# Latent mixer: who settles the steps of a bisection, and who copies one transposed piece in four

## The chip, the cores and the metric

One Trainium2 chip, one of its cores. The metric is the device time of one execution in microseconds; lower is better. TensorE multiplies and transposes, VectorE (DVE), ScalarE (ACT) and GpSimd (POOL) work on tiles of 128 partitions, and SyncE (SP) issues transfers here. Each engine runs its own list of instructions in order; semaphores order them between engines. GpSimd reads SBUF alone, the other three read PSUM too.

## The reference

One inference step of a two-layer encoder for a prompt of 1024 frames and a sample of 64 frames over a cache of 256. Layer 0 has two head groups side by side: A, attention over keys that an indexer selects, and B, multi-head latent attention. What matters here:

```python
def mla_core(k_nope, k_rope, v, k_pos, q_nope, q_rope, q_pos):      # group B, the latent mixer
    logits = (einsum('bqhd,bshd->bhqs', q_nope, k_nope)
              + einsum('bqhd,bsd->bhqs', q_rope, k_rope)) * (B_NOPE + B_ROPE) ** -0.5
    logits = where(chunk_mask(q_pos, k_pos)[None, None], logits, -inf)
    p = softmax(logits, axis=-1)
    return einsum('bhqs,bshd->bqhd', p, v)                          # 8 heads, k_nope and v = latent @ w_ukv

def dsa_core(...):                                                  # group A
    idx_score = einsum('bqhs,bqh->bqs', relu(sc), wi)               # masked
    _, sel = top_k(idx_score, topk)                                 # 256 of up to 1024 keys
    ...                                                             # attention over the selected keys
```

## The kernel before

The program is a row of stages, one behind the other: the projection of layer 0, the indexer's scores, the latent mixer (`attention` with kind "b", tiles `att_b_...`), the sparse mixer ("a"), output projection, the two halves of the feed-forward block, and then layer 1. A stage begins when the one before it has ended on all engines.

**Units.** The latent mixer works through 36 units: four pairs of heads, and in each pair nine query tiles t = 0 to 8. Tile t < 8 has 128 queries and 128 (t + 1) keys; tile 8 is the sample, 64 queries and 320 keys. A unit's width is its number of keys, so t = 4 to 7, with five to eight blocks of 128 keys, are the wide units. Per unit and head:

- TensorE computes the scores into PSUM (`scores`, L1128), three units ahead (`ahead` = 3).
- VectorE masks them, copies them to `prob` and takes the row's extreme (`peak`, L1362).
- ScalarE takes the exponential with its sum (`exponential`, L1291).
- VectorE takes the reciprocal of the sum (`over_sum`, L1385).
- GpSimd scales the row by it in place (L1103), which is the normalising.
- TensorE transposes the row, block by block, into one of three PSUM banks (`piece`, L1167): group 0 is blocks 0 to 3, group 1 blocks 4 to 7. The order in a unit is group 0 of head 0, group 0 of head 1, group 1 of head 0, group 1 of head 1. A piece waits until the piece three places before it has been copied out.
- An engine copies each piece to SBUF (`copy_piece`, L1226 on ScalarE, tile `pt`). `copier` says who: for the latent mixer always ScalarE.
- TensorE multiplies with the values (`products`, L1196) for the unit before, and ScalarE takes the result away (`output`, L1281).

During a pair TensorE also expands the next pair's keys and values from the latents (`expand`, L1147 and L1151, kind "x"), through the same three banks, in order behind the unit's transposed pieces; ScalarE copies those with even numbers and VectorE those with odd numbers. The last pair has none.

**The search.** The indexer's scores of six query tiles (t = 2 to 7) lie in SBUF, and the sparse mixer needs for each row the value of its 256th largest. It is found by bisection on the bits of a float: 32 steps, spread over the first 30 units by `search_steps`, one to a unit and two in units 16 and 25 (t = 7 of the second and the third pair, the doubled units). In a step VectorE counts for three tiles how many scores lie below the candidate (L1417, 896, 768 and 512 columns), and ScalarE for the other three by a sum of signs (L1298, 1024, 640 and 384 columns). `settle` then compares six counts per partition with their limits, keeps the candidate's bit or not, and writes the next candidate (L1424, L1427, L1432, all 128x6). The next count on both engines waits for `cand_ready`. VectorE's order in a unit is: over_sum(i + 1, head 1), in a doubled unit the first count, two peaks for unit i + 3, in a doubled unit the first settling, its expanded pieces, the count, over_sum(i + 2, head 0), settle. ScalarE's is: output, copies of group 0, an exponential, in a doubled unit the first count, copies of group 1, an exponential, its expanded piece, the count. GpSimd has nothing but the normalising, head 0 and then head 1.

**The tail.** From unit 30 on VectorE turns the bits found into thresholds and masks (`next_float`, `room_for_ties`, `select`), and works through four of the six tiles in units 32 to 35.

## Time and profile before

| what | us |
|---|---|
| median of 3 runs | 3007.72 (3005.83 to 3008.99) |
| the profiled execution | 3008.22 |
| its span | 3006.4 |
| TensorE busy | 2833.9 (94%) |
| VectorE busy | 2018.3 (67%) |
| ScalarE busy | 1412.2 (47%) |
| GpSimd busy | 532.4 (18%) |

The shares are averages over all stages. The change touches one stage, so the whole program's shares say little about it: its own windows have to be read. A time of the timeline counts from the span's start. "Idle before" in a row is the time the engine stood still ahead of that instruction, with what ended it. The ends of matrix multiplications are modelled, and the durations of GpSimd are rough; distances between starts are firmer.

### The profile page before, as it was taken

How to read it: one execution, taken by the hardware profiler on the slowest of the kernel's cores; microseconds unless marked ns; L12 is line 12 of the kernel's file. 1: busy time of each engine (PE TensorE's matmuls, PEld its weight loads, DVE VectorE, ACT ScalarE, POOL GpSimd, SP SyncE). 2: the span in 40 equal slices, each digit the busy share in tenths (PEclk: the TensorE clock that was granted, in tenths of full speed). 3: DMA queues.
4: the chain of work that ended last, by engine and by line, in shares of the span. 5: the costliest groups of instructions: out<-in, count | busy, mean ns of one | idle time of the engine just before them, and what ended most of it. 6: DMA issues, size and time to landing. Idle time of an engine off the chain costs nothing. (4 is left out here: it accounts for less than half of the span.)

```text
span 3006.4 us, 49479 instructions
## 1 busy us (share of the span) xinstructions
PE 2833.9 (94%) x18462; PEld 2368.9 (79%) x18462; DVE 2018.3 (67%) x3648; ACT 1412.2 (47%) x2850; POOL 532.4 (18%) x410
## 2 busy tenths in 40 slices
PE   8986997999999999899999899999899999999998
PEld 6762564668899999788799566865688999998787
DVE  5447999865867776677631565139857777767777
ACT  5335996552444344433243455348724444444333
POOL 0000222420011110465000231000000111114551
PEclk9996999999999999999999999999999999999999
DMA  4111001021233323654411201120112333326442
GB/s 154 46 36 29 14 14 50 2 65 67 75 97 104 107 97 96 235 172 129 168 51 46 92 2 53 56 77 2 58 74 61 101 109 99 104 91 227 154 130 103
DMA packets 203120, 259.04 MB, mean 86 GB/s; under 512 B 27100, under 2 KB 132180, under 8 KB 202900
## 3 DMA queue, kind: packets, MB, share of 16 engines
q1 hardware_dynamic: 202900, 256.10, 25.8%
q8 instruction: 139, 2.28, 0.3%
q14 instruction: 81, 0.66, 0.1%
HBM read 177.90 MB, written 77.64 MB: 85 GB/s over the span
## 5 line engine op out<-in xcount | busy, mean ns | idle before, releaser
L247 PE MATMUL X<-up_th,high 128*128 128x272 f32 x1232 | 356.4, 289 | 4.1 <-ACT up_U L2287 2.9
L249 PE MATMUL X<-up_th,low_r 128*128 128x272 f32 x1232 | 355.2, 288 | 0.0
L247 PEld LDWEIGHTS X<-up_th,high 128*128 128x128 f32 x1232 | 232.2, 188 | 8.3 <-ACT up_U L2287 6.1
L2248 POOL TENSOR_TENSOR up_sum<-up_U 128x512 f32<-128x512 f32 x20 | 33.4, 1669 | 1131.9 <-DVE up_U L2399 1131.9
L249 PEld LDWEIGHTS X<-up_th,low_r 128*128 128x128 f32 x1232 | 231.9, 188 | 0.0
L2381 DVE SCALAR_TENSOR_TENSOR up_cv<-up_G,tap,up_cv 128x1024 f32<-128x1024 f32 (+1 forms) x176 | 130.3, 782 | 136.9 <-ACT up_cv L2296 135.3
L247 PE MATMUL up_x<-up_th,up_high 128*128 128x272 f32 x704 | 202.9, 288 | 1.4 <-DVE up_low_r L1859 1.4
L249 PE MATMUL up_x<-up_th,up_low_r 128*128 128x272 f32 x704 | 203.7, 289 | 0.0
L248 PE MATMUL X<-sums_r,high 128*128 128x272 f32 x528 | 152.0, 288 | 0.0
L247 PE MATMUL up_y<-up_th,up_high 128*128 128x272 f32 x528 | 151.9, 288 | 0.0
L249 PE MATMUL up_y<-up_th,up_low_r 128*128 128x272 f32 x528 | 151.6, 287 | 0.0
L2795 DVE TENSOR_TENSOR xres<-X,xres 128x1024 f32<-128x1024 f32 x80 | 97.4, 1222 | 72.1 <-PE X L249 72.1
L247 PE MATMUL X<-w_hi_p_r,a_hi_p_r 128*128 128x512 f32 x352 | 137.9, 392 | 0.0
L249 PE MATMUL X<-w_hi_p_r,a_lo_p_r 128*128 128x512 f32 x352 | 137.8, 391 | 0.0
L248 PE MATMUL X<-w_lo_p_r,a_hi_p_r 128*128 128x512 f32 x352 | 137.7, 391 | 0.0
L247 PEld LDWEIGHTS up_x<-up_th,up_high 128*128 128x128 f32 x704 | 132.9, 189 | 1.8 <-DVE up_low_r L1859 1.8
L2692 ACT ACTIVATE w_hi_p_r<-b_f 128x1024 fp32r<-128x1024 f32 x54 | 57.0, 1056 | 161.0 <-POOL b_f L2751 41.9
L249 PEld LDWEIGHTS up_x<-up_th,up_low_r 128*128 128x128 f32 x704 | 132.5, 188 | 0.0
L2770 DVE TENSOR_TENSOR a_lo_p_r<-a_lo_p_f,a_hi_p_r 128x1024 fp32r<-128x1024 f32 x64 | 107.6, 1689 | 10.6 <-ACT a_hi_p_r L2696 10.6
L1859 DVE TENSOR_TENSOR up_low_r<-up_low,up_high 128x1024 fp32r<-128x1024 f32 (+1 forms) x66 | 109.9, 1664 | 1.3 <-ACT up_high L1849 0.6
L1849 ACT ACTIVATE up_high<-up_low 128x1024 fp32r<-128x1024 f32 (+1 forms) x66 | 79.2, 1203 | 64.2 <-DVE up_low L1840 64.2
L2736 POOL TENSOR_TENSOR w_lo_p_r<-b_f,w_hi_p_r 128x1024 fp32r<-128x1024 f32 x38 | 102.2, 2692 | 37.1 <-ACT w_hi_p_r L2692 37.0
(581 smaller groups left out, 8665.6 us busy)
## 6 DMA issues: line engine op xcount, KB each, us to landing
scratch_a<-up_U SPq DMA_DIRECT2D x44, 544.0 KB, 2.7
low<-in_w_up_dram SPq DMA_DIRECT2D x44, 512.0 KB, 5.1
up_low<-in_w_up_dram SPq DMA_DIRECT2D x44, 512.0 KB, 4.9
scratch_s<-up_sum SPq DMA_DIRECT2D x80, 256.0 KB, 2.0
b_f<-in_w_down_dram SPq DMA_DIRECT2D x40, 512.0 KB, 4.4
a_lo_p_f<-scratch_s SPq DMA_DIRECT2D x40, 512.0 KB, 4.2
a_lo_p_f<-scratch_a SPq DMA_DIRECT2D x30, 512.0 KB, 4.5
scratch_att<-out_x SPq DMA_DIRECT2D x16, 512.0 KB, 2.6
```

Source lines behind the costliest of these rows:

```text
L247: nc.tensor.matmul(out, lh, rh, start=first, stop=False, skip_group_check=on_top)
L248: nc.tensor.matmul(out, lh, rl, start=False, stop=False, skip_group_check=on_top)
L249: return nc.tensor.matmul(out, ll, rh, start=False, stop=last, skip_group_check=on_top)
L1849: nc.scalar.activation(high[:, j0:j1], raw[:, j0:j1], ACT.Copy).then_inc(hi, 1)
L1859: nc.vector.tensor_tensor(low[1][:, j0:j1], low[0][:, j0:j1], high[:, j0:j1].bitcast(F32), ALU.subtract).then_inc(lo, 1)
L2248: g.tensor_tensor(t0, a21, a22, ALU.add).then_inc(pair_summed, 1)
L2381: last = v.scalar_tensor_tensor(cv[:, t0:t0 + n], G[m % 2][:, g0 + j:g0 + j + n], tap[:, j * NF + m:j * NF + m + 1], cv[:, t0:t0 + n], ALU ...
L2692: s_.activation(slots.split(f"w_hi_{what}"), w_source(what), ACT.Copy).then_inc(w_hi, 1)
L2736: g.tensor_tensor(slots.split(f"w_lo_{what}"), w_source(what), slots.high(f"w_hi_{what}"), ALU.subtract).then_inc(w_lo_pool, 1)
L2770: v.tensor_tensor(slots.split(f"{x}_lo_{what}"), of, slots.high(f"{x}_hi_{what}"), ALU.subtract).then_inc(lo, 1)
L2795: v.tensor_tensor(xs, bank[:, 2 * h:2 * h + 2, :], xs, ALU.add).then_inc(added, 1)
```

## The change

`settle` moves from VectorE's list to GpSimd's. There it follows the normalising of the next unit: behind the two scalings of unit i stand the settlings of the steps of unit i - 1. The exclusive-or, the predicated copy and the shift to a constant are replaced by arithmetic: the difference between limit and count (`room`, in the tile `ok`) is compared with zero, the result is multiplied by a signed step `flip` and added to `bits`, `flip` is halved, and the next candidate is `bits` plus `flip`. After the first step that is six instructions of 128x6 instead of three. The first step sets `bits` and `flip` in its own way. `settled` counts four a step instead of two, a semaphore `flipped` and a tile `flip` are new, and VectorE waits for the last settling before `next_float`.

In `copier`, for the latent mixer, the piece of head 1 and group 1 goes to VectorE: the last transposed piece of every wide unit. In VectorE's list these copies are the first instruction of the unit, ahead of over_sum(i + 1, head 1).

```diff
--- before.py
+++ after.py
@@ -977,7 +977,9 @@
 
         if what == "x":
             return "dve" if j % 2 else "act"
-        if mla or stick:
+        if mla:
+            return "dve" if (x, j) == (1, 1) else "act"
+        if stick:
             return "act"
         return "act" if x == 0 else "dve"
 
@@ -995,7 +997,8 @@
             below = sb("below", [P, wide[-1]], BF16)
             up = sb("up", [P, n_top], mybir.dt.int32)
             counted = {"dve": sem("counted_dve"), "act": sem("counted_act")}
-            settled, cand_ready = sem("settled"), sem("cand_ready")
+            flip = sb("flip", [P, n_top], mybir.dt.int32)
+            settled, cand_ready, flipped = sem("settled"), sem("cand_ready"), sem("flipped")
         if mla or dsa:
             top, work, spare, told = src["top"], src["work"], src["top"]["spare"], sem("told")
             scratch = below if mla else sb("scratch", [P, 2 * SEQ], BF16)
@@ -1094,6 +1097,31 @@
                     for h in range(2):
                         g.memset(left[s][h][:, SEQ:SEQ + 1], 1.0).then_inc(cleared, 1)
                 return
+            def settle(step):
+
+                for by, n in (("dve", BY_DVE), ("act", n_top - BY_DVE)):
+                    pool.wait_ge(counted[by], FROM + n * (step + 1))
+                room = top["ok"][:].bitcast(F32)
+                g.tensor_tensor(room, top["limit"][:], top["cnt"][:], ALU.subtract).then_inc(settled, 1)
+                pool.wait_ge(settled, FROM + 4 * step + 1)
+                if step:
+                    g.tensor_scalar(top["cand"][:], room, 0.0, None, ALU.is_ge).then_inc(settled, 1)
+                    pool.wait_ge(settled, FROM + 4 * step + 2)
+                    g.tensor_tensor(top["cand"][:], top["cand"][:], flip[:], ALU.mult).then_inc(settled, 1)
+                    pool.wait_ge(settled, FROM + 4 * step + 3)
+                    g.tensor_tensor(top["bits"][:], top["bits"][:], top["cand"][:], ALU.add).then_inc(settled, 1)
+                    if step + 1 < STEPS:
+                        g.tensor_scalar(flip[:], flip[:], 0.5, None, ALU.mult).then_inc(flipped, 1)
+                else:
+                    g.tensor_scalar(top["bits"][:], room, 0.0, 1.0, ALU.is_ge, ALU.subtract).then_inc(settled, 2)
+                    g.tensor_scalar(flip[:], room, 0.0, 2.0, ALU.is_ge, ALU.mult).then_inc(settled, 1)
+                    pool.wait_ge(settled, FROM + 4)
+                    g.tensor_scalar(flip[:], flip[:], 1.0, float(1 << 30), ALU.subtract, ALU.mult).then_inc(flipped, 1)
+                if step + 1 < STEPS:
+                    pool.wait_ge(settled, FROM + 4 * step + 4)
+                    pool.wait_ge(flipped, FROM + step + 1)
+                    g.tensor_tensor(top["cand"][:], top["bits"][:], flip[:], ALU.add).then_inc(cand_ready, 1)
+
             for i, (p, t) in enumerate(order):
                 n, w = queries(t), key_tile(t)[0]
                 for h in range(2):
@@ -1101,6 +1129,9 @@
                     c = 2 * (i % ring) + h
                     pool.wait_ge(rcp_done[h], FROM + i + 1)
                     g.tensor_scalar(pr, pr, rr[0:n, c:c + 1], 1.0, ALU.mult, ALU.mult).then_inc(prob_ready[h], 1)
+                if mla and i:
+                    for step in SEARCH_AT[i - 1]:
+                        settle(step)
 
         @block.tensor
         def _(pe):
@@ -1417,20 +1448,6 @@
                     v_.tensor_scalar(below[:, wide[j]:wide[j + 1]], w[:], top["cand"][:, j:j + 1].bitcast(F32), None, ALU.is_lt, ALU.add,
                                      accum_out=top["cnt"][:, j:j + 1]).then_inc(counted["dve"], 1)
 
-            def settle(step):
-
-                for by, n in (("dve", BY_DVE), ("act", n_top - BY_DVE)):
-                    dve.wait_ge(counted[by], FROM + n * (step + 1))
-                v_.tensor_tensor(top["ok"][:], top["cnt"][:], top["limit"][:], ALU.is_le).then_inc(settled, 1)
-                dve.wait_ge(settled, FROM + 2 * step + 1)
-                if step:
-                    v_.copy_predicated(top["bits"][:], top["ok"][:], top["cand"][:]).then_inc(settled, 1)
-                else:
-                    v_.tensor_scalar(top["bits"][:], top["ok"][:], 1.0, None, ALU.subtract).then_inc(settled, 1)
-                dve.wait_ge(settled, FROM + 2 * step + 2)
-                if step + 1 < STEPS:
-                    v_.tensor_scalar(top["cand"][:], top["bits"][:], 1 << (30 - step), None, ALU.bitwise_xor).then_inc(cand_ready, 1)
-
             def not_above(columns):
                 for j in columns:
                     w = work[SEARCHED[j]]
@@ -1517,8 +1534,6 @@
                 if i + ahead < n_units:
                     for h in range(2):
                         peak(i + ahead, h)
-                if mla and len(SEARCH_AT[i]) > 1:
-                    settle(SEARCH_AT[i][0])
                 if i:
                     pieces_of(dve, "dve", i, "x")
                     if not mla:
@@ -1531,9 +1546,8 @@
                     count_below(SEARCH_AT[i][-1])
                 if i + 2 < n_units:
                     over_sum(i + 2, 0)
-                if mla and SEARCH_AT[i]:
-                    settle(SEARCH_AT[i][-1])
                 if mla and i == SEARCH_ENDS + 1:
+                    dve.wait_ge(settled, FROM + 4 * STEPS)
                     next_float()
                 if mla and i == SEARCH_ENDS + 2:
                     room_for_ties()
```

## Rows read from the trace of the kernel before

**Rows 1.** Windows of the search and the tail, all engines, busy us (instructions).
```profile
308.00:476.20 168.20, 152.36 (x1014) 97.15 (x1013) 160.04 (x476) 166.71 (x446) 42.02 (x58) 0.98 0.05 13
...
476.20:508.00 31.80, 23.95 (x226) 16.33 (x224) 31.17 (x68) 16.60 (x43) 9.45 (x10) 1.00 0.00 1
```

**Rows 2.** Waits of ScalarE in the search: us in total, times, longest.
```profile
ACT att_b_k L1226 <- PE att_b_tp L1147: 1.0, 3, 0.7
```

**Rows 3.** Timeline, first count end and count starts: start us, duration us.
```profile
311.56 0.08 DVE L1417 DVE_READ_ACCUMULATOR att_b_below<-scores,top_cand 128x1 f32 x1
...
312.76 1.15 ACT L1298 ACTIVATE att_b_below<-scores,top_cand 128x1024 bf16<-128x1024 f32 x1
...
393.16 1.14 ACT L1298 ACTIVATE att_b_below<-scores,top_cand 128x1024 bf16<-128x1024 f32 x1
...
397.19 1.15 ACT L1298 ACTIVATE att_b_below<-scores,top_cand 128x1024 bf16<-128x1024 f32 x1
...
401.07 1.15 ACT L1298 ACTIVATE att_b_below<-scores,top_cand 128x1024 bf16<-128x1024 f32 x1
...
405.70 1.18 ACT L1298 ACTIVATE att_b_below<-scores,top_cand 128x1024 bf16<-128x1024 f32 x1
...
409.91 1.18 ACT L1298 ACTIVATE att_b_below<-scores,top_cand 128x1024 bf16<-128x1024 f32 x1
```

**Rows 4.** Timeline of step 12, VectorE and GpSimd.
```profile
375.36 1.13 DVE L1417 TENSOR_SCALAR_CACHE_REDUCE att_b_below<-scores,top_cand 128x896 bf16<-128x896 f32 x1
...
378.02 0.07 DVE L1417 DVE_READ_ACCUMULATOR att_b_below<-scores,top_cand 128x1 f32 x1
...
378.26 0.93 POOL L1103 TENSOR_SCALAR att_b_prob<-att_b_prob,att_b_rr 128x768 f32<-128x768 f32 x1 [4.48 <-DVE att_b_rr L1385]
...
378.53 0.68 DVE L1432 TENSOR_SCALAR top_cand<-top_bits 128x6 int32<-128x6 int32 x1
```

**Rows 5.** Groups of GpSimd (busy us, mean ns, idle), then its timeline.
```profile
L1103 POOL TENSOR_SCALAR att_b_prob<-att_b_prob,att_b_rr 128x128 f32<-128x128 f32 x8 | 3.0, 376 | 29.4 <-DVE att_b_rr L1385 29.4
...
L2759 POOL TENSOR_TENSOR b_f<-b_f,b_f 128x1024 f32<-128x1024 f32 x10 | 24.0, 2396 | 0.0
...
L3099 POOL MEMSET const-float32-1.0<- 128x1 f32 x1 | 0.1, 98 | 0.0
...
820.92 1.66 POOL L2248 TENSOR_TENSOR up_sum<-up_U 128x512 f32<-128x512 f32 x1 [177.70 <-DVE up_U L2399]
...
822.73 1.56 POOL L2251 TENSOR_TENSOR up_sum<-up_sum,up_U 128x512 f32<-128x512 f32 x1
...
826.40 1.29 POOL L2257 TENSOR_TENSOR up_sum<-up_U 128x512 f32<-128x512 f32 x1 [0.42 <-DMA scratch_s<-up_sum]
```

**Rows 6.** Timeline of the second pair's unit with five blocks.
```profile
370.59 0.32 ACT L1298 ACTIVATION_READ_ACCUMULATOR att_b_below<-scores,top_cand 128x1 f32 x1
...
372.98 0.80 POOL L1103 TENSOR_SCALAR att_b_prob<-att_b_prob,att_b_rr 128x640 f32<-128x640 f32 x1 [0.17 <-DVE att_b_rr L1385]
...
374.03 1.09 PE L1167 MATMUL att_b_tp<-ident,att_b_prob 128*128 128x128 f32 x8
```

**Rows 7.** Copies of transposed pieces: timeline of ScalarE, group of VectorE (sparse mixer).
```profile
399.74 1.07 ACT L1226 ACTIVATE att_b_pt<-att_b_tp 128x512 f32<-128x512 f32 x2
...
L1250 DVE COPY att_a_pt<-att_a_tp 128x512 f32<-128x512 f32 x24 | 16.3, 680 | 5.2 <-PE att_a_tp L1167 5.2
```

**Rows 8.** Timeline of the first pair's unit with eight blocks.
```profile
346.71 0.15 DVE L1385 RECIPROCAL att_b_rr<-att_b_rs 64x1 f32<-64x1 f32 x1
...
346.82 0.66 PE L1167 MATMUL att_b_tp<-ident,att_b_prob 128*128 128x128 f32 x4 [0.56 <-ACT att_b_pt L1226]
...
348.50 0.69 DVE L1237 COPY att_b_v<-att_b_tp 128x512 f32<-128x512 f32 x1 [0.84 <-PE att_b_tp L1151]
```

**Rows 9.** Timeline at the end of the search.
```profile
474.52 0.26 ACT L1298 ACTIVATION_READ_ACCUMULATOR att_b_below<-scores,top_cand 128x1 f32 x1
...
476.09 0.08 DVE L1417 DVE_READ_ACCUMULATOR att_b_below<-scores,top_cand 128x1 f32 x1
```

## The prediction

> **What bounds the kernel now.** The change lies inside one stage, the latent mixer, which runs from about 298 to 508 us; the stages before and after it keep their instructions, so its length is all that can move. I cut the stage by windows first. While the search runs (308 to 476 us) ScalarE is busy 166.71 of 168.20 us and VectorE 160.04, GpSimd only 42.02 [rows 1]. In the tail (476 to 508) ScalarE is half idle and VectorE is busy 31.17 of 31.80 us [rows 1]. The list of waits says the same in another way: through the search ScalarE's longest entry is 1.0 us in three waits, for TensorE's block of expanded keys that it copies, and it never waited for a candidate [rows 2]. So ScalarE's own work sets the pace of the search, VectorE comes close behind, and the tail is VectorE's alone.
>
> Then I read the search step by step. Both engines count against one candidate, the step is settled, and both count again. The starts of ScalarE's first count in five successive steps, 393.16 to 409.91 [rows 3], are the loop. From the unit with seven blocks into the doubled unit they are 4.03 us apart, inside it 3.88, then 4.63 and 4.21; 168 us for 31 intervals make 5.4 on average. The reader is to see that these four intervals are short: they leave little between the end of one count and the start of the next for anything that must happen in between.
>
> **Settling.** Removed from VectorE: three instructions a step, 96 in all less one. In step 12 the last read of the count starts at 378.02 and the candidate write, held up beside a normalising instruction of GpSimd (378.26 to 379.19), ends at 379.21 [rows 4]: 1.1 us from the end of a count to a candidate, less where the normalising is narrow. VectorE sheds 0.6 to 1.1 us a step, some 25 us. That buys nothing by itself, because ScalarE sets the pace.
>
> Added to GpSimd: in each step after the first subtract, compare, multiply, add, halve the flip, add the next candidate. Five of these six form a chain through semaphores; the halving sits in GpSimd's order before the last. The trace has none of them at 6 columns. A one-source instruction costs 0.38 us at 128 columns [rows 5] and 0.93 at 768 [rows 4]: 0.55/640 = 0.86 ns a column, so 0.27 fixed. A two-source one costs 1.29 us at 512 columns at best and 2.40 at 1024: 2.16 ns a column, so 0.19 fixed; the slower form at 512 (1.66) gives 0.55 [rows 5]. I take 0.30, nearer the clean pair. A GpSimd instruction that waits for the one before it starts 0.15 us after its end (820.92 + 1.66 to 822.73) [rows 5]; the first wait, for the count, I put at 0.1 and the last, GpSimd to another engine, at 0.15. The chain: 0.1 + (0.30 + 0.15) + (0.27 + 0.15) + (0.30 + 0.15) + 0.30 + 0.27 (halving) + 0.15 + 0.30 + 0.15 = 2.6; the halving overlaps the add's end a little, so 2.5 us. From below, with 0.19 for the four, it is 2.0; from above, with 0.55, 3.4. No row is a 6-column operation: the nearest tiny one, a memset of one column, shows 0.10 [rows 5]; with 0.10 for all six the chain is 1.4. That is the bottom of the range.
>
> The Trainium skill (GPSIMD Engine Reference, Performance versus the Vector engine) gives 4497 ns for a two-source add of 2048 columns at 2.6 cycles a column of 1.2 GHz; an estimate from it leaves 0.06 us fixed. By that page the chain would be about 1.5 us instead of 2.5, and the sum below about +1 instead of +13. No row here shows which holds at 6 columns.
>
> VectorE's three counts take 2.73 us (375.36 to 378.09) [rows 4]. Both engines wait for the same candidate, so no two starts can be closer than 2.73 + 2.5, some 5.24 us. Against [rows 3]: 4.03 loses 1.21, 3.88 loses 1.36, 4.63 loses 0.61, 4.21 loses 1.03, together 4.21. The same four stand at the end of the third head pair: 4.21 again. The first pair has no doubled unit, so only the last two: 1.64. Other intervals are long enough, or nearly. The very first step: VectorE's count ends at 311.64, a candidate comes at 314.1 at the earliest, ScalarE wants it at 312.76 [rows 3]: 1.3. Sum **+11.4 us**. With a chain of 2.0 the same working gives 6 (2.2 twice, 0.6, 0.9). With 3.4 the loop is 6.14, above the average interval: 23 by these places alone, and some 7 in the intervals up to 6.14.
>
> **Normalising behind it.** GpSimd works in order: the scaling of unit i+2 is queued behind the settling of unit i, so it starts a chain later than the count's end, where before it started 0.2 us after it; the second head was held until VectorE had settled (1.2 us after), so it comes 1 to 1.5 us later than now. What waits for it is TensorE's transposition, then scores, then the expanded keys, then ScalarE's copy of them. Where ScalarE waits for that copy now, there is no cover: the three waits of [rows 2], one in the five-block unit of each pair. There the second head is scaled from 372.98 for 0.80, and TensorE turns both heads in eight transpositions from 374.03 to 375.12, the second head's from the middle, 374.55 [rows 6]. With the change ScalarE's count ends at 370.91 [rows 6], the chain at 373.4, the first head takes 0.95 to the start of the second, which ends at 375.15 and is handed over at 375.3: 0.8 late, and ScalarE comes a little earlier than now. I take 0.9, three pairs, **2.7**. The third unit of the search, right behind the late first candidate, I take at 1.0 more. Together **+3.7**; 1.5 if TensorE has more room than its modelled ends show, 6 if the third unit of the later pairs falls behind too. The DMAs of the stage are issued from SP's queue and are not moved.
>
> **The copy on VectorE.** Sixteen pieces, in each pair one of 128, 256, 384 and 512 columns. ScalarE has two of 512 in 1.07 us [rows 7], so about 0.5 each and, by columns, 1.25 a pair, 3.8 in the three pairs of the search. The three of 128 columns sit ahead of the wait for TensorE and are given back as wait: **-3.3 us**. VectorE pays 0.68 for 512 [rows 7], 1.7 to 1.9 a pair, well inside what it sheds. But its instruction stands first in the unit, and the reciprocal, the next score maxima and the count are queued behind it. In the first pair's unit with eight blocks VectorE starts with the reciprocal at 346.71, waits 0.84 before its key copy at 348.50, which ends at 349.19; TensorE has the piece only at 346.82 to 347.48 [rows 8]. With the change VectorE waits, copies to 348.15, and needs 0.95 of work and the key copy: its count starts near 349.7, 0.6 later, and the loop passes it on. The doubled units I take at 0.2 each: **+1.0**.
>
> **Tail.** Four more copies on the engine that sets it: +1.7. But VectorE's last count ended at 476.17, ScalarE's at 474.78 [rows 9]; this lag of 1.4 and the last settling (0.4) go. **About 0.**
>
> **Sum.** 11.4 + 3.7 - 3.3 + 1.0 + 0 = 12.8. The profiled execution took 3008.22 us (span 3006.4), 0.5 more than the median of the runs: 3021.0, or 3020.5 beside the median. I say 3021.
>
> **Rivals.**
> - *Cheap settling.* A tiny GpSimd operation costs nearer the memset's 0.10, chain 1.4 to 1.9. The loop is then 4.1 to 4.6: it loses 0.6 to 4; normalising is 0.3 to 0.9 late, +1 to +2; -3.3 for copies, +0.6 for waits. -1 to +3, so 3007 to 3011. For it: the page's figure above. Against: each one-source read by GpSimd fits a line with 0.27 fixed.
> - *All hidden, faster.* ScalarE loses the copies (-3.8) and its waits (1.0), VectorE's lag at the end goes: 3001 to 3003. It decides if count end to candidate stays under 1.2 us, the room in the doubled unit (3.88 - 2.73). The three settling instructions of VectorE just make it; GpSimd's six would need 0.1 each with waits included.
> - *The dear chain.* Two-source operations at 0.55 fixed, chain 3.4: +30, 3038.
> - *TensorE as the bound.* If both heads' lateness reaches ScalarE in every unit before a wide one, +6 instead of +3.7, and idle TensorE may be granted less clock: 3025 to 3030.
>
> **How the numbers follow.** About 0.2%, 6 us, is what a measurement of this kernel tells from no change. My sum 0.55 (3013 to 3028, of a chain 2.0 to 2.9); dear chain 0.10; TensorE 0.12; cheap settling 0.18; all hidden 0.05. Slower: the first three, 0.77. Same: 0.18. Faster by over 0.2%: only the most complete hiding with something I have not seen, 0.05. The range leaves out half of the dear chain and the hidden case: 3006 to 3033; that of my sum alone is 3013 to 3028.
>
> **What would show it.** In the profile after: ScalarE's waits for GpSimd's candidate at some ten places, up to 1.4 us each; the four intervals of [rows 3] all near 5.2 us; GpSimd's chain from count end to candidate at 2.5; VectorE idle by 15 to 25 us more in the search; ScalarE's wait on the expanded keys near 1 us in the five-block units; GpSimd with 190 more instructions. A chain under 1.5 us would make the prediction wrong, so would TensorE's copies waiting nowhere.

## The result and the profile after

| what | before | after |
|---|---|---|
| median of 14 runs each | 3007.64 | 3016.45 |
| the profiled execution | 3008.22 | 3016.93 |
| its span | 3006.4 | 3015.1 |
| latent mixer, first start to last end of its `att_b_...` instructions | 214.67 | 220.25 |
| sparse mixer, the same of `att_a_...` (same instructions in both) | 141.89 | 143.39 |

The kernel is slower by 0.27%: ratio 1.0027, interval 1.0020 to 1.0034. That is 8.8 us; I had predicted 12.8 more than the profiled execution and a range of 3006 to 3033. Two of the 14 runs of the kernel before (3958.73 and 6797.40 us) lie far off and are left out of the ratio.

A second series of the changed kernel gave 1.0026 (1.0017 to 1.0036), with medians 7.0 us apart (3014.47 against 3007.50), and its profiled execution repeats both stage lengths: 220.32 and 143.36. So 5.6 us belong to the latent mixer and 1.5 to the stage behind it, 7.1 together. In the rest no effect of the change shows: it took 2649.9 us before, and 2651.5 and 2647.5 in the two profiles after.

First the windows of the changed kernel, all engines: window, its length, then busy us with instructions for PE, PEld, DVE, ACT and POOL, the granted TensorE clock, the DMA share and GB/s.

```profile
308.00:480.00 172.00, 150.12 (x1010) 94.93 (x1010) 142.57 (x393) 163.25 (x433) 78.88 (x243) 0.98 0.05 13
410.00:414.00 4.00, 2.41 (x18) 1.62 (x18) 3.47 (x11) 3.85 (x13) 2.16 (x8) 0.80 0.01 2
414.00:418.00 4.00, 4.00 (x13) 1.80 (x12) 2.04 (x7) 2.73 (x10) 2.38 (x8) 0.77 0.02 4
480.00:514.20 34.20, 27.12 (x230) 18.67 (x228) 32.06 (x72) 16.81 (x42) 11.59 (x14) 0.95 0.00 1
```

Two of these windows in the kernel before:

```profile
410.00:414.00 4.00, 3.99 (x16) 2.08 (x17) 3.93 (x13) 4.00 (x13) 0.56 (x1) 1.00 0.01 2
414.00:418.00 4.00, 3.71 (x16) 2.02 (x15) 4.00 (x10) 4.00 (x12) 0.64 (x2) 1.00 0.03 6
```

Beside [rows 1] the reader is to see three things. VectorE is idle for 29 us of the search, where it was for 8. ScalarE, which had stood still for 1.5 us in 168, now does so for 8.75 in 172: it still sets the pace, but it waits. And the granted clock is 0.80 and 0.77 in two windows, 410 to 414 and 414 to 418, where the kernel before had 1.00 in both: one stretch at the lower of the two levels, 1.2 GHz, lies across them (0.50 in 412.5 to 415.5). A second such stretch lies in the next pair of heads (0.50 in 467.2 to 470.2). The mean of the clock over the search is 0.98 in both kernels, for the kernel before has low windows too, elsewhere (0.72 in 390 to 396, 0.86 in 438 to 450); what counts is whether somebody waits for TensorE there. The second profile of the changed kernel, whose stage starts 2.6 us earlier, has 0.81 and 0.77 at the same place (407.4 to 411.4 and 411.4 to 415.4).

Then the waits of the search: ScalarE's three, the first two of TensorE; total, times, longest.

```profile
ACT att_b_below L1329 <- POOL top_cand L1123: 5.4, 9, 1.2
ACT att_b_k L1257 <- PE att_b_tp L1178: 2.9, 4, 1.3
ACT att_b_v L1257 <- PE att_b_tp L1182: 0.3, 1, 0.3
PE att_b_tp L1198 <- POOL att_b_prob L1131: 10.1, 10, 1.7
PE att_b_tp L1198 <- ACT att_b_pt L1257: 7.3, 11, 1.3
```

ScalarE waits 8.6 us, before 1.4 (with the 1.0 of [rows 2] a single wait of 0.4 for expanded values): 7.2 more. From the start of its first count to the end of its last it is busy 2.7 us less (162.7 instead of 165.4), and this stretch grows by 4.6. VectorE, which had ended 1.3 us behind ScalarE, now ends with it, so the search grows by less: VectorE's last count ends at 480.09 instead of 476.17 [rows 9], 3.9 later, of which 0.6 is the later start of the stage. The tail grew from 31.8 to 34.1 us, 2.3 more. With 3.3 that makes 5.6.

**The chain.** GpSimd's groups in the search, by shape: busy us, mean ns of one, then idle before.

```profile
L1114 POOL TENSOR_SCALAR att_b_flip<-att_b_flip 128x6 int32<-128x6 int32 x30 | 7.3, 244 | 0.0
L1108 POOL TENSOR_SCALAR top_cand<-top_ok 128x6 int32<-128x6 f32 x30 | 7.1, 238 | 2.8
L1105 POOL TENSOR_TENSOR top_ok<-top_limit,top_cnt 128x6 f32<-128x6 f32 x31 | 6.2, 199 | 79.7 <-DVE att_b_below L1448 59.4 <-ACT att_b_below L1329 20.3
L1123 POOL TENSOR_TENSOR top_cand<-top_bits,att_b_flip 128x6 int32<-128x6 int32 x31 | 6.1, 196 | 4.6
```

And one settling in the timeline, from VectorE's last read to the next count of both engines.

```profile
400.89 0.07 DVE L1448 DVE_READ_ACCUMULATOR att_b_below<-scores,top_cand 128x1 f32 x1
401.05 0.20 POOL L1105 TENSOR_TENSOR top_ok<-top_limit,top_cnt 128x6 f32<-128x6 f32 x1 [2.06 <-DVE att_b_below L1448]
401.35 0.24 POOL L1108 TENSOR_SCALAR top_cand<-top_ok 128x6 int32<-128x6 f32 x1
401.67 0.20 POOL L1110 TENSOR_TENSOR top_cand<-top_cand,att_b_flip 128x6 int32<-128x6 int32 x1
401.94 0.20 POOL L1112 TENSOR_TENSOR top_bits<-top_bits,top_cand 128x6 int32<-128x6 int32 x1
402.11 0.24 POOL L1114 TENSOR_SCALAR att_b_flip<-att_b_flip 128x6 int32<-128x6 int32 x1
402.50 0.20 POOL L1123 TENSOR_TENSOR top_cand<-top_bits,att_b_flip 128x6 int32<-128x6 int32 x1
402.73 1.15 ACT L1329 ACTIVATE att_b_below<-scores,top_cand 128x1024 bf16<-128x1024 f32 x1 [1.21 <-POOL top_cand L1123]
402.73 1.15 DVE L1448 TENSOR_SCALAR_CACHE_REDUCE att_b_below<-scores,top_cand 128x896 bf16<-128x896 f32 x1 [0.47 <-POOL top_cand L1123]
```

From the end of the last read, 400.96, to the end of the candidate, 402.70, are 1.74 us. A small operation that waits for the one before starts 0.27 to 0.32 us after that one's start: 0.20 or 0.24 of work and 0.07 to 0.10 of handing over. Only the last, which waits for the halved flip, starts 0.15 after the end of the halving. I had 2.5 us, and 0.15 for each handing over. The loop is then 2.73 us of counting (VectorE's three counts, as in the prediction) and 1.75 of chain, some 4.5 us.

**TensorE.** The unit with two blocks in the third pair of heads: the count behind it, TensorE's transpositions of its rows and the score products behind them, in the changed kernel and then in the kernel before.

```profile
411.86 1.15 ACT L1329 ACTIVATE att_b_below<-scores,top_cand 128x1024 bf16<-128x1024 f32 x1
...
412.43 1.12 PE L1198 MATMUL att_b_tp<-ident,att_b_prob 128*128 128x128 f32 x4 [1.47 <-POOL att_b_prob L1131]
...
413.34 3.56 PE L1159 MATMUL att_b_s<-att_b_k,q 96*128 96x512 f32 x8
...
417.83 0.54 ACT L1257 ACTIVATE att_b_k<-att_b_tp 64x448 f32<-64x448 f32 x1 [1.27 <-PE att_b_tp L1178]
...
418.27 1.14 ACT L1329 ACTIVATE att_b_below<-scores,top_cand 128x1024 bf16<-128x1024 f32 x1
```
```profile
410.01 0.41 PE L1167 MATMUL att_b_tp<-ident,att_b_prob 128*128 128x128 f32 x2 [0.34 <-POOL att_b_prob L1103]
...
410.25 2.33 PE L1128 MATMUL att_b_s<-att_b_k,q 96*128 96x512 f32 x8
```

The normalising comes behind the chain, TensorE stands still for 1.47 us, and the eight score products behind it take 3.56 us; before, TensorE had waited 0.34 and the same eight took 2.33. ScalarE waits 1.27 us for the expanded key at the end of this, and its two count starts are 6.41 us apart instead of 5.00 (409.91 to 414.91). This one place costs 1.4 us, a quarter of what the stage grew by. In the fourth pair the same wait (1.48 us at 467.01) again has eight products of 3.57 us behind it; there VectorE waits 1.98 us for the scores, the step is settled late and the interval grows by 1.2 us. In the second pair the wait is as long, but the clock stays at 1.00:

```profile
359.27 0.87 PE L1198 MATMUL att_b_tp<-ident,att_b_prob 128*128 128x128 f32 x4 [1.52 <-POOL att_b_prob L1131]
359.98 2.33 PE L1159 MATMUL att_b_s<-att_b_k,q 96*128 96x512 f32 x8
```

The products take 2.33 us as before, and ScalarE's counts are 5.02 us apart where they were 5.00. So what costs here is the slow clock behind the wait and not the wait.

**Behind the stage.** The start of the sparse mixer, changed kernel: its window of 5.6 us, five filler products that both kernels have there, and its first scores. Then the same products in the kernel before.

```profile
514.45:520.05 5.60, 4.15 (x15) 1.73 (x15) 1.59 (x11) 1.69 (x8) 1.00 (x3) 0.70 0.47 121
```
```profile
514.48 2.02 PE L264 MATMUL att_a_o<-ident_bf 128*128 128x512 bf16 x5 [2.00 <-PEq L57]
516.42 1.65 PE L1159 MATMUL att_a_s<-kaT,qaT 64*128 64x128 f32 x8
517.25 0.29 DVE L1393 CUSTOM_DVE_ANT_0 att_a_prob<-att_a_s,bias 128x128 f32<-128x128 f32 x1 [3.10 <-PE att_a_s L1159]
```
```profile
508.27 1.24 PE L264 MATMUL att_a_o<-ident_bf 128*128 128x512 bf16 x5 [2.46 <-PEq L57]
509.44 0.93 PE L1128 MATMUL att_a_s<-kaT,qaT 64*128 64x128 f32 x8
```

Before, the clock of this window was 1.00 and VectorE waited 2.01. The two groups take 0.8 and 0.7 us longer after, and the stage is 1.5 us longer. The lower clock isn't brought over from the latent mixer, whose last 12.9 us ran at 1.00: it falls just behind the start of a stage that the diff does not touch (0.50 in 515 to 518), where before it fell 5.8 us into it (0.50 in 514.2 to 517.2).

### The profile page after: what moved, and what is told of

Its sections match the earlier page's. It is cut to its first block and busy times, and to the rows that moved or that the text cites. A ratio compares the mean times of both kernels' runs of the same rounds, so it can differ in the third digit from the quotient of the medians.

```text
span 3015.1 us, 49606 instructions
## 1 busy us (share of the span) xinstructions
PE 2837.8 (94%) x18462; PEld 2372.3 (79%) x18462; DVE 1993.8 (66%) x3569; ACT 1408.3 (47%) x2834; POOL 574.1 (19%) x599
## 5 line engine op out<-in xcount | busy, mean ns | idle before, releaser
L247 PE MATMUL out_mm<-out_whi,out_ahi 128*128 128x512 f32 x256 | 103.2, 403 | 6.0 <-DVE wo_odd_r L1986 3.0
```

The costliest lines, as they stand in the source:

```text
L247: nc.tensor.matmul(out, lh, rh, start=first, stop=False, skip_group_check=on_top)
```

## The experiments

Ratios are against the kernel before, timed beside them; medians of different series are not compared. Stage lengths (latent mixer 214.67 before, 220.25 after) are from one profiled execution each. As the two profiles after agree within 0.1 us on this length, it tells more of the stage than the whole time does.

| kernel | ratio (interval) | median | latent mixer | sparse mixer |
|---|---|---|---|---|
| the change | 1.0027 (1.0020 to 1.0034) | 3016.45 | 220.25 | 143.39 |
| settling alone | 1.0030 (1.0018 to 1.0042) | 3017.41 | 222.88 | 143.52 |
| copies alone | 1.0010 (1.0001 to 1.0019) | 3011.34 | 216.16 | 144.21 |
| shorter chain | 1.0014 (1.0005 to 1.0023) | 3012.38 | 218.28 | 142.03 |
| longer chain | 1.0056 (1.0041 to 1.0070) | 3028.17 | 230.93 | 141.74 |
| filler on TensorE | 1.0006 (0.9997 to 1.0015) | 3009.33 | 217.79 | 141.93 |
| same filler, kernel before | 0.9998 (0.9989 to 1.0007) | 3007.53 | 215.42 | 142.42 |
| settling between the heads | 1.0041 (1.0027 to 1.0056) | 3018.81 | 227.95 | 142.12 |
| copy behind the maxima | 1.0019 (1.0010 to 1.0028) | 3013.03 | 218.38 | 142.06 |
| three repairs | 1.0003 (0.9994 to 1.0012) | 3007.11 | 215.15 | 142.38 |
| and keys to VectorE | 0.9988 (0.9979 to 0.9997) | 3004.08 | 210.57 | 141.91 |
| and copy behind the maxima | 0.9980 (0.9970 to 0.9989) | 3002.19 | 209.99 | 141.73 |

**Settling alone.** The changed kernel without its copies.

```diff
-        if mla:
-            return "dve" if (x, j) == (1, 1) else "act"
-        if stick:
+        if mla or stick:
```

> Settling on GpSimd, every transposed piece copied by ScalarE as before. Chain theory (the loss comes from the longer way from a count's end to the next candidate in the short intervals, and from the scaling queued behind it; the moved copies are worth about 3 us in the search and cost 1.7 us in the tail): the stage gets no shorter than with both edits, 5.6 us over the kernel before plus 3.3 less 1 less 1.7, so +6; the program +8 to +10. Copy theory (VectorE's wait for the piece at the head of its unit is the loss): most of it goes, stage +0 to +3, program +2 to +5. The candidate is still written about 1.73 us after a count's end in both.

Measured: 1.0030, stage 222.88, which is 8.2 over before. The settling alone loses more than both edits together, and 2 us more than I had expected. ScalarE waits for the expanded keys 4.1 us, five times, and for candidates 2.3; the two lines of the search:

```profile
ACT att_b_k L1255 <- PE att_b_tp L1176: 4.1, 5, 1.5
ACT att_b_below L1327 <- POOL top_cand L1121: 2.3, 6, 0.5
```

With the copies still on ScalarE, ScalarE comes later to its count and covers more of the chain, so of the two prices TensorE's lateness is here the larger one. The granted clock over the search was 0.95.

**Copies alone.** The kernel before with the new rule of `copier`.

```diff
-        if mla or stick:
+        if mla:
+            return "dve" if (x, j) == (1, 1) else "act"
+        if stick:
```

> The last piece of each wide unit copied by VectorE, settling on VectorE as before. Chain theory: ScalarE's list is 3.8 us shorter in the search, but VectorE's, which was busy 160 of 168 us, gets 5 us more and waits for TensorE's piece; neither dominates, stage +1 to +5. Copy theory: VectorE's waits in the units of six, seven and eight blocks are the loss, stage +6 or more. A third view, that the copy alone is the useful half: stage -2 to -4.

Measured: 1.0010, stage 216.16, 1.5 over before. What ScalarE sheds it waits for elsewhere:

```profile
ACT att_b_below L1300 <- DVE top_cand L1434: 2.4, 2, 1.4
ACT att_b_k L1228 <- PE att_b_tp L1149: 1.8, 3, 0.8
```

VectorE was busy 160 of 168 us, and is busy 167.24 of 172 here: it settles too, and comes late with the candidate. The copies pay only where VectorE has been relieved first: on top of the settling the same edit takes 2.6 us off the stage (222.88 to 220.25).

**A shorter chain.** Half of `flip`, and `bits` plus that half, are made before the counts arrive; from count to candidate there are then four operations instead of six.

```diff
+                if step and not last:
...
+                    g.tensor_scalar(pick, flip[:], 0.5, None, ALU.mult).then_inc(flipped, 1)
+                    pool.wait_ge(flipped, FROM + 2 * step)
+                    g.tensor_tensor(base, top["bits"][:], pick, ALU.add).then_inc(based, 1)
...
+                    if not last:
+                        g.tensor_tensor(top["cand"][:], base, pick, ALU.add).then_inc(cand_ready, 1)
+                    g.tensor_tensor(top["bits"][:], top["bits"][:], pick, ALU.add).then_inc(settled, 1)
```

> As the changed kernel, but GpSimd prepares bits plus half the flip before it waits for the counts, so that four instructions and not six stand between the counts and the candidate; the work is the same, two instructions a step more. The tiles up and top_spare hold the intermediates. Chain theory: count end to candidate 1.2 us instead of 1.73, the loop in the short intervals 4.0 instead of 4.53, and GpSimd is free for the scaling a little earlier; stage 3 to 4 us shorter than with the change, program +4 to +6 over the kernel before. Copy theory: no change beside the changed kernel, +8 to +9.

Measured: 1.0014, stage 218.28, 2.0 under the change and not 3 to 4. The first and the last of the four operations of one step:

```profile
394.69 0.20 POOL L1115 TENSOR_TENSOR top_ok<-top_limit,top_cnt 128x6 f32<-128x6 f32 x1 [1.48 <-ACT att_b_below L1339]
...
395.58 0.20 POOL L1123 TENSOR_TENSOR top_cand<-top_spare,att_b_up 128x6 int32<-128x6 int32 x1
```

From the subtraction's start to the candidate's are 0.89 us instead of 1.45. ScalarE's wait for candidates falls from 5.4 to 3.0. But its wait for expanded keys grows from 2.9 to 4.2, and here is why:

```profile
410.00:414.00 4.00, 3.88 (x10) 1.94 (x11) 2.03 (x8) 4.00 (x13) 2.29 (x10) 0.67 0.00 0
414.00:418.00 4.00, 4.00 (x12) 1.64 (x10) 1.70 (x5) 1.75 (x6) 1.22 (x4) 0.50 0.00 0
```

At 0.50 TensorE is at 1.2 GHz throughout. It is busy 4.00 of 4.00 us and ScalarE is idle for more than half: in these 4 us TensorE is the bound.

**A longer chain.** Two additions whose results nothing uses, each waiting for the one before, ahead of the candidate.

```diff
+                    for x in range(2):
+                        pool.wait_ge(padded, FROM + 2 * step + x)
+                        g.tensor_tensor(idle[:], idle[:] if x or step else top["bits"][:], flip[:], ALU.add).then_inc(padded, 1)
+                    pool.wait_ge(padded, FROM + 2 * step + 2)
```

> As the changed kernel, with two more dependent GpSimd additions a step ahead of the candidate, on a tile that is not used otherwise. Chain theory: the chain grows from 1.73 to about 2.3 us, the loop from 4.53 to 5.1; with the scaling behind it the stage loses 0.56 us at some 12 to 16 places, 6 to 9 us over the changed kernel, program +15 to +18 over the kernel before. Copy theory: at most 2 us more.

Measured: 1.0056, stage 230.93, 10.7 over the change, above the 6 to 9 expected. One step, from the subtraction to the candidate:

```profile
395.44 0.20 POOL L1106 TENSOR_TENSOR top_ok<-top_limit,top_cnt 128x6 f32<-128x6 f32 x1 [1.88 <-ACT att_b_below L1334]
...
397.44 0.20 POOL L1128 TENSOR_TENSOR top_cand<-top_bits,att_b_flip 128x6 int32<-128x6 int32 x1
```

The chain is 2.00 us between these starts, 0.55 longer than 1.45. A chain shorter by as much had given back only 2.0. So the price is not a straight line. By the places (the table in the next part): in the ten short intervals the longer chain costs 5.0 us more and the shorter one gives back 2.1, since there is no more to win where the counts no longer wait for it. The first two intervals take 2.3 more with the longer chain, and the clock is low there too (0.50 in 316 to 319); how much of this is the clock was not isolated. ScalarE waits 10.6 us for candidates (13 times) and 5.2 for keys.

**Filler on TensorE.** Five multiplications of 128x512 in bf16, whose results nothing uses, ahead of the first transposition in the two narrowest units of the second to the fourth pair. They fill the time in which TensorE waits for the normalised rows.

```diff
+                    if mla and i > TILES - 1 and order[i][1] in (0, 1) and (a, j) == (0, 0):
+                        spin(nc, tp[:], consts, 5)
                     pe.wait_ge(prob_ready[a], FROM + i + 1)
```

> As the changed kernel, with five extra 128x512 bf16 multiplications on TensorE ahead of the first transposition in the units of one and two blocks from the second pair on, where it waits up to 1.5 us for GpSimd's scaling; they go into a bank that is free and add nothing to the result. Clock theory (while it waits for the scaling queued behind the settling, TensorE is granted the lower clock, and the scores behind that wait take twice as long): granted clock 1.0 there instead of 0.63 to 0.80, ScalarE's 1.3 us wait for expanded keys and VectorE's 2 us waits for scores at those places shrink, stage 1 to 3 us shorter than with the change. Chain theory alone (only GpSimd's instructions count): no change beside the changed kernel, or up to 1 us longer.

Measured: 1.0006, stage 217.79, 2.5 under the change with the same chain. The search, and the places of the lower clock:

```profile
308.00:480.00 172.00, 154.48 (x1058) 97.39 (x1056) 144.08 (x397) 165.68 (x438) 81.61 (x249) 1.00 0.05 13
...
410.00:414.00 4.00, 3.89 (x25) 1.98 (x24) 3.52 (x10) 3.85 (x12) 1.81 (x7) 1.00 0.02 6
414.00:418.00 4.00, 4.00 (x21) 2.29 (x20) 3.20 (x8) 4.00 (x11) 2.31 (x8) 1.00 0.00 0
```

The granted clock is back at 1.00, the wait for keys falls from 2.9 to 1.5 and that for candidates from 5.4 to 4.3. Laid interval by interval beside the changed kernel, ScalarE's counts differ at the two places told above, in the third and the fourth pair: there the 1.4 and the 1.2 us are gone. No other interval of the search moves by more than 0.1. The sparse mixer is back at 141.93 too, and the clock at its start at 1.00.

**The same filler in the kernel before.**

> The kernel before with the same five extra multiplications in the units of one and two blocks. If the extra multiplications repair what the change spoils (TensorE waits 2.2 us for GpSimd in the kernel before and its clock is 1.00 in these units): no gain here, -1 to +2 us. If they help whatever the settling does: 2 us or more faster, and g1's gain says nothing of the change.

Measured: 0.9998, stage 215.42. The filler is worth nothing there, so what it mends came with the change. It left the low window of 390 to 396 as it was (0.72), where ScalarE of the kernel before did not wait; it brought that of 438 to 450 from 0.86 to 1.00; and in the second pair it makes TensorE late, which costs one interval 0.9 us. The second series of the changed kernel ran beside it:

> The changed kernel once more, beside e7 and k1 on one chip. The first profile showed 3.1 us of its 8.7 outside the latent mixer, in stages whose instructions are the same. If that belongs to the change, the stages outside take 2795 us again; if it is the spread of executions, they come out anywhere between 2789 and 2797 as in the other profiles, and the stage itself at 220 to 221 again.

Measured: 1.0026, stage 220.32. Outside the latent mixer it took 2790.8 us, where the first profile had 2794.9 and the kernel before 2791.8: most of the 3.1 us is the spread of executions, and only the 1.5 of the sparse mixer come again.

**Settling between the heads.** The settling stands between the two scalings of the unit after next, so that head 0 is normalised first (in the doubled units the first of the two stays where it was).

```diff
                     g.tensor_scalar(pr, pr, rr[0:n, c:c + 1], 1.0, ALU.mult, ALU.mult).then_inc(prob_ready[h], 1)
+                    if mla and i > 1 and not h:
+                        for step in SEARCH_AT[i - 2][-1:]:
+                            settle(step)
                 if mla and i:
-                    for step in SEARCH_AT[i - 1]:
+                    for step in SEARCH_AT[i - 1][:-1]:
                         settle(step)
```

> As the changed kernel, with the settling moved one place in GpSimd's list: it stands behind the scaling of the first head of the unit after next instead of ahead of it. Scaling theory (what counts is that TensorE gets its rows late): TensorE's wait for GpSimd falls from 10 us, stage 1 to 3 us shorter. Candidate theory: the scaling of 0.37 to 1.13 us now stands between the counts and the candidate, the loop in the short intervals grows from 4.53 to 4.9 to 5.1, stage 2 to 5 us longer.

Measured: 1.0041, stage 227.95, 7.7 over the change, more than either theory had. Two scalings and what stands between them:

```profile
392.89 1.12 POOL L1131 TENSOR_SCALAR att_b_prob<-att_b_prob,att_b_rr 128x1024 f32<-128x1024 f32 x1 [1.97 <-DVE att_b_rr L1419]
393.98 0.20 POOL L1105 TENSOR_TENSOR top_ok<-top_limit,top_cnt 128x6 f32<-128x6 f32 x1
...
395.44 0.20 POOL L1123 TENSOR_TENSOR top_cand<-top_bits,att_b_flip 128x6 int32<-128x6 int32 x1
395.62 1.13 POOL L1131 TENSOR_SCALAR att_b_prob<-att_b_prob,att_b_rr 128x1024 f32<-128x1024 f32 x1
```

The subtraction waits for a scaling of 1.1 us: ScalarE's last read ended at 393.13, the candidate at 395.64, 2.5 us later. ScalarE waits 9.0 us for candidates, 14 times, and TensorE waits for GpSimd as long as in the change (10.7 against 10.1). Normalising head 0 first bought TensorE nothing and cost the candidate up to a scaling. So the order that the change chose, candidate first, is the better one.

**The copy behind the maxima.** VectorE's copy of the piece stands behind over_sum and the two maxima, not first in the unit.

```diff
+                if not mla:
+                    for c in range(2):
+                        pieces_of(dve, "dve", i, "t", c)
...
+                if mla:
+                    for c in range(2):
+                        pieces_of(dve, "dve", i, "t", c)
                 if i:
                     pieces_of(dve, "dve", i, "x")
```

> As the changed kernel, with VectorE's copy of the transposed piece behind its two score maxima and no longer at the head of the unit. Copy theory (VectorE waits 13.7 us for this piece in nine places): the waits fall to a few us and the stage gets 3 us shorter or more. Chain theory: VectorE has that time to spare except in the first pair's unit of eight blocks and the doubled units, 0 to 2 us shorter.

Measured: 1.0019, stage 218.38, 1.9 under the change. The wait of VectorE for the piece falls from 13.7 us in nine waits to 5.3 in four; TensorE waits for GpSimd 6.5 instead of 10.1. But only 0.6 of the 1.9 us come from the ten short intervals, where the wait was to cost; 1.6 come from the narrow units, and there the clock is another one too (1.00 in 410 to 418, while its mean over the search is 0.95). The reciprocal that GpSimd's scaling of head 1 needs stands behind that copy in the change and ahead of it here, which fits; it was not tried by itself.

**Repairs together.** The shorter chain, the filler, and the last pair's copies on ScalarE; then also the expanded pieces with even numbers, but number 6, to VectorE in the later pairs; then also the copy behind the maxima.

```diff
-                by = copier(*what)
+                by = "act" if expands and what[0] == "t" and p == PAIRS - 1 else copier(*what)
...
-            return "dve" if j % 2 else "act"
+            return "dve" if j % 2 or (x and j != 6) else "act"
```

> The prepared base of f1, the extra multiplications, and in the last pair of heads all copies back on ScalarE, where VectorE sets the end. If the three causes add: chain 1.2 instead of 1.73 us (worth 2 to 4), clock (1 to 2), tail copies (1.7): stage 213 to 215 us, as long as before or 1 us shorter, program -2 to +2. If they hide behind one another, stage 216 to 218.

> As h1, with VectorE also copying the expanded keys and values with even numbers of the later pairs (all but number 6), so that ScalarE, which sets the pace, has some 6 us less. If ScalarE's list is what bounds the search once the chain is short: stage 3 to 5 us shorter than h1, 209 to 212 us, program 2 to 5 us faster than before. If VectorE's waits for TensorE have become the bound: no shorter than h1.

> h2 with the copy behind the maxima as well. If the head of VectorE's unit delays the count in the doubled units (0.4 to 1 us each, which ScalarE then waits for): stage 1 to 2 us shorter than h2, 209 us, program 4 to 6 us faster than before. If the later copy holds TensorE's bank instead: as long as h2 or 1 to 2 us longer.

Measured: stages 215.15, 210.57 and 209.99, and ratios 1.0003, 0.9988 and 0.9980. With the three repairs the change costs nothing and brings nothing. Handing the keys over takes another 4.6 us off the stage: that is what the time freed on VectorE is good for. Handing them over in the kernel before was not tried; the copies alone, given to a VectorE that was busy 160 of 168 us, had lost 1.5. The last version beats the kernel before by 0.2% (median 3002.19 against 3007.50). The later copy gave 0.6 us of the stage and not 1 to 2. The search of the last version:

```profile
308.00:480.00 172.00, 159.44 (x1096) 101.15 (x1095) 156.30 (x431) 164.64 (x434) 94.18 (x312) 1.00 0.05 13
```

VectorE works 156.30 of 172 us instead of 142.57, and the clock is 1.00.

## Why the prediction held, and where its working did not

The direction, the place and the order of size were right. The terms for the chain and for the normalising were far too large, the lower clock of TensorE was missing, and the total profited from errors of opposite sign.

The starts of ScalarE's first counts cut the search into 31 intervals, and each can be laid beside its own in the kernel before. "Ten short" are the intervals that the prediction named, four in each of the second and third pair and two in the first; "three narrow" end at 362.65, 414.91 and 472.07 us in the kernel before, where the units with one to three blocks are at work. The last column but one runs from ScalarE's last count to the end of the stage.

| us over the kernel before | first two | ten short | three narrow | other sixteen | end | stage |
|---|---|---|---|---|---|---|
| the change | 0.7 | 4.5 | 2.6 | -3.2 | 1.0 | 5.6 |
| settling alone | 0.7 | 3.3 | 5.2 | -0.8 | -0.2 | 8.2 |
| copies alone | 0.0 | 2.2 | 0.0 | -2.1 | 1.4 | 1.5 |
| shorter chain | 0.6 | 2.4 | 2.5 | -2.8 | 0.8 | 3.6 |
| longer chain | 3.0 | 9.5 | 3.0 | -1.5 | 2.2 | 16.3 |
| filler on TensorE | 0.7 | 4.6 | 0.1 | -3.1 | 0.7 | 3.1 |
| copy behind the maxima | 0.7 | 3.9 | 1.1 | -3.2 | 1.2 | 3.7 |

**The chain (2.5 us, +11.4).** Mis-sized. It is 1.74 us, below even my lower bound of 2.0 from fitted lines, though above the 1.4 that the one-column memset would give. My fixed cost of 0.27 for a one-source operation was close (0.24); 0.30 for a two-source one was the wrong pick, 0.19 from the clean pair was right (0.20); and 0.15 for a handing over, read behind an operation of 1.66 us, is 0.07 to 0.10 behind a small one. So the four intervals of [rows 3] are 4.50, 4.73, 4.64 and 4.49 us (count starts 393.50 to 411.86), not 5.2, and ScalarE waits 5.4 us for candidates at nine places, up to 1.2; one of these, 1.1 us, is the late settling of the fourth pair behind TensorE's slow products. I had named ten places and up to 1.4 us. (Two other signs came as written: VectorE idle for 21 us more in the search, and GpSimd with 185 more instructions.) Where I had 10.1 us for the ten short intervals and 1.3 for the first step, they grew by 4.5 and 0.7.

The Trainium skill (GPSIMD Engine Reference, Performance versus the Vector engine) gave me an estimate of 0.06 us fixed. The trace does not agree: 0.20 us at 6 columns. I had taken the handing over as too dear, the estimate from the page is too cheap, and the chain lies between the 1.5 and the 2.5 that I had from them.

**Normalising behind it (+3.7).** Mis-sized, and the larger price was another one. TensorE does wait for GpSimd 10.1 us instead of 2.2, and what reaches ScalarE is the wait for the expanded key. But in the three five-block units, for which I had 0.9 us each, these waits grew only from 1.0 to 1.6 us together (0.35, 0.59 and 0.65), and the third unit of the search lost 0.2 instead of 1.0. The fourth and longest wait, 1.27 us, stands in the two-block unit of the third pair, for which I had nothing, and is the clock's. I had let TensorE keep its clock. That belonged to a rival with 0.12, and it came true in part: with the filler the stage loses 2.5 us and the one behind it 1.5. Of the 7.1 us that the two stages grew by, the filler takes back 4.0. It changes nothing else in the order of the work, and gives the kernel before nothing.

**The copies (-3.3) and the wait ahead of them (+1.0).** Both near. ScalarE gives away 12 copies in the search and is busy 2.7 us less there (4.2 less than with the settling alone); against the settling alone the other sixteen intervals shorten by 2.4 us. VectorE stands 13.7 us before these copies, but little of it counts: against the settling alone the ten short intervals grow by 1.2, against the copy behind the maxima by 0.6.

**Tail (about 0).** Too low: +1.0. From VectorE's last count to the end are 2.3 us more, and my figure had counted against the copies that VectorE's lag behind ScalarE goes away, which is 1.3 of it. Without the copies (settling alone) that stretch grew by 0.9 only, so some 1.4 go with them; I had 1.7. And VectorE now waits for scores where the last count had covered that:

```profile
480.01 0.08 DVE L1448 DVE_READ_ACCUMULATOR att_b_below<-scores,top_cand 128x1 f32 x1
...
481.81 1.09 DVE L1393 CUSTOM_DVE_ANT_0 att_b_prob<-att_b_s,att_b_hidden 128x896 f32<-128x896 f32 x1 [1.57 <-PE att_b_s L1159]
```

The lag went (ScalarE's last read begins at 479.79, VectorE's at 480.01), but TensorE was not ready sooner. The clock has its part: 0.95 over 480 to 514.2, with 0.74 in 498 to 504, where [rows 1] has 1.00. How much of the rest is its part is not settled.

**The length of one stage is all that can move.** Wrong by 1.5 us, through the clock in the first microseconds of the next stage. All kernels whose window there shows 0.99 or 1.00 have a sparse mixer of 141.7 to 142.1 us; with 0.60 to 0.70 it is 142.4 to 144.2. Among the latter are also the kernel before with filler (0.63, 142.42) and the copies alone (0.70, 144.21), so the settling is not the only thing that moves a stretch of low clock there; what moves it was not isolated.

**What the total owes to luck.** With a chain of 1.75 my working gives about +2 (2.9 for the short intervals, 0.6 for the first step, some 0.7 for the normalising, -3.3 and +1.0); it was 7.1 in the two stages. What is left are the three terms that it lacked: 2.6 in the narrow units, which the filler takes away, 1.0 in the tail and 1.5 in the sparse mixer. With the longer chain, 2.3 us, the same working gives about +10, and 16.3 us were measured in the stage. So 12.8 came near 8.8 because a chain that was too long stood in for a clock that I had left out. The rival of cheap settling had the chain right (1.4 to 1.9) and the time wrong (3007 to 3011), because it too let TensorE keep its clock and had nothing for the tail.

**What stays open.** The filler and the windows show that the clock falls behind some of TensorE's waits, and that this costs time; why it falls behind the waits of 1.47 and 1.48 us and not behind that of 1.52 they don't show. Each variant but the change was profiled once, so a difference of a microsecond between two variants is less sure than the table looks. The settling alone has the clock at 1.00 in 410 to 414 and 0.67 in 414 to 418, the longer chain 0.50 and 0.93 there. A version without the chain at all, with TensorE's waits as they are, was not tried.

## What to carry to other kernels

Moving a chain of small dependent steps to an idle engine pays only if the chain, handings over included, fits the room between the end of one round and the start of the next on the engine that sets the pace; count that room first (here 1.2 us, against 1.74), and what stands in order behind the chain. An engine that is relieved brings nothing until work of the bound is given to it, and such work should not stand first in its unit if it waits. Where matrix work waits a microsecond more, look at the granted clock in the windows behind it, and in the next stage, before pricing the wait: here a wait of 1.5 us cost nothing at 1.00 and 1.2 to 1.4 us where the clock fell. And lay the same intervals of two kernels side by side; the mean clock was 0.98 in both and told nothing.

## What the runs showed of the hardware

- GpSimd on 128x6: 0.20 us for a two-source operation, 0.24 for a one-source one; a dependent one starts 0.27 to 0.32 us after the start of the one before (0.39 for the last of the chain). Independent neighbours start 0.17 us apart (401.94 to 402.11), less than one of them lasts.
- Two waits of TensorE of 1.47 and 1.48 us stand ahead of a stretch at a granted clock of 0.50, in which eight products of 96x512 take 3.56 us instead of 2.33; behind a wait of 1.52 us of the same kind the clock was 1.00 and they took 2.33. Five filler products of 128x512 at six places brought the whole search from 0.98 to 1.00.
- The place of low clock can move in a stage with the same instructions: in the sparse mixer it began 5.8 us behind the start before and within 0.6 us after, and the first eight products took 1.65 us instead of 0.93 (a factor 1.8).
